# Streaming a two-layer transformer's weight matmuls backwards, with interleaved stationary columns

## What is computed

```
proj = rmsnorm(x) @ w_in                    # 2048 x 7184, then the two mixers
x = x + mixed @ w_out
x = x + cross_attention(rmsnorm(x), rmsnorm(mem), w_xq, w_xkv, w_xo)
x = x + conv_ffn(rmsnorm(x), w_up, w_down)  # 2048 x 11264, 5632 x 2048
p = rmsnorm(x) @ fox_w_in; x = x + (fox_attention(p) * silu(gate)) @ fox_w_out
p = rmsnorm(x) @ swa_w_in; x = x + (swa_attention(p) * silu(gate)) @ swa_w_out
```

## Time and profile before

| | |
|---|---|
| runs | 2170.38, 2169.81, 2169.99 us |
| median | 2169.99 us |
| profiled execution | span 2167.6 us from its first to its last instruction; what lies around the span is the 2.4 us to the median |
| TensorE busy | 2156.3 us, 99% |
| weight loads busy | 1865.8 us, 86% (beside the matmuls) |
| VectorE, ScalarE busy | 75%, 61% |
| DMA | 389 MB, mean 180 GB/s |

### The profile page before, as it was taken

How to read it: one execution, slowest core, us unless ns; L and a number is a source line. 1 busy time by engine, 2 the same in 40 slices (tenths; PEclk the granted TensorE clock), 3 DMA queues, 4 the chain that set the end, 5 groups by cost and what they waited for, 6 DMA issues and landing times.

```text
span 2167.6 us, 34503 instructions
## 1 busy us (share of the span) xinstructions
PE 2156.3 (99%) x13406; PEld 1865.8 (86%) x13406; DVE 1618.3 (75%) x2945; ACT 1327.2 (61%) x2601; POOL 9.7 (0%) x22
## 2 busy tenths in 40 slices
PE   9999999999999999999999999999999999999998
PEld 8888888888888888888888888888888888888887
DVE  7898666786688877655778867777676767688774
ACT  7866447775576666544666656555556655567764
POOL 0000000000000000000000000000000000000000
PEclk9999999999999999999999999999999999999999
DMA  7443434665455555555555555545554455544453
GB/s 279 169 146 137 147 115 141 218 217 186 156 190 189 188 191 186 193 185 192 187 191 189 185 194 185 193 171 197 181 177 174 167 192 186 189 161 155 146 200 140
DMA packets 107619, 389.31 MB, mean 180 GB/s; under 512 B 12304, under 2 KB 12560, under 8 KB 106688
## 3 DMA queue, kind: packets, MB, share of 16 engines
q1 hardware_dynamic: 105264, 377.31, 50.2%
q0 software_dynamic: 1904, 9.47, 1.2%
q10 hardware_dynamic: 288, 0.32, 0.0%
HBM read 384.34 MB, written 2.13 MB: 178 GB/s over the span
## 4 chain that ended last, share of the span: by engine, by line
PE 95%; DVE 3%; ACT 1%; issue 0%; DMA 0%; SPq 0%; DVEq 0%; ACTq 0%
PE main L510 88%; PE two L510 6%; PE two L513 1%; DVE WL L987 1%; DVE gt L987 0%; DMA RAW<-ws 0%; DVE GQ L993 0%; ACT L1654 0%; ACT WH L1655 0%; DVE GK L993 0%; PE main L556 0%; ACT PP L1655 0%; DVE PB L987 0%; ACT NT L1655 0%; DVE PP L993 0%
## 5 line engine op out<-in xcount | busy, mean ns | idle before, releaser
L1655 ACT ACTIVATE WH<-RAW 128x512 fp32r<-128x512 f32 x1416 | 882.1, 629 | 657.6 <-PE main L510 651.1
L987 DVE TENSOR_TENSOR WL<-RAW,WH 128x512 fp32r<-128x512 f32 x1416 | 961.2, 687 | 383.9 <-ACT WH L1655 374.4
L510 PE MATMUL main<-A,WH 128*128 128x512 f32 (+1 forms) x3680 | 1141.9, 393 | 1.0 <-DVE WL L987 1.0
L510 PEld LDWEIGHTS main<-A,WL 128*128 128x128 f32 x3584 | 673.9, 188 | 154.8
L510 PE MATMUL main<-A,WL 128*128 128x256 f32 x3584 | 713.7, 278 | 0.0
L510 PEld LDWEIGHTS main<-A,WH 128*128 128x128 f32 x3680 | 562.7, 189 | 13.8 <-issue 9.3
L510 PE MATMUL main<-H,WH 128*128 128x512 f32 x704 | 221.1, 395 | 0.0
L510 PE MATMUL main<-B,WH 128*128 128x512 f32 (+1 forms) x640 | 184.4, 373 | 0.0
L510 PEld LDWEIGHTS main<-H,WL 128*128 128x128 f32 x704 | 132.3, 188 | 31.3
L510 PE MATMUL main<-H,WL 128*128 128x256 f32 x704 | 138.4, 278 | 0.0
L510 PE MATMUL main<-WH,A 128*128 128x512 f32 (+1 forms) x448 | 137.6, 380 | 0.0
(11 more groups left out here) (322 smaller groups left out, 1722.5 us busy)
## 6 DMA issues: line engine op xcount, KB each, us to landing
RAW<-ws SPq DMA_DIRECT2D x707, 512.0 KB, 3.3
CB<-cscr POOLq DMA_DIRECT2D x4, 1024.0 KB, 4.7
XT<-xT POOLq DMA_DIRECT2D x4, 512.0 KB, 6.0
MS<-memT POOLq DMA_DIRECT2D x4, 512.0 KB, 8.7
xs<-xT SPq DMA_DIRECT2D x7, 256.0 KB, 7.6
out<-YT SPq DMA_DIRECT2D x7, 256.0 KB, 2.6
CST<-cst SPq DMA_DIRECT2D x1, 1248.0 KB, 7.9
G<-g POOLq DMA_DIRECT2D x1, 1024.0 KB, 5.9
```

Source lines behind the costliest of these rows:

```text
L510: return e.matmul(o, l, r, start=start, stop=True, skip_group_check=True)
L987: return e.tensor_tensor(o, a, b, op)
L1655: return e.activation(o, i, f, bias=bias, scale=scale, accum_out=accum)
```

## The change

`back` reverses the moving operand and the result of a matmul along their columns, and replaces `mm` in every matmul of `main(j)` except the transposes of `w2*`. Both are reversed, so each result column lands where it did. In the forms other than tokens, a stationary operand is now every second column of a block of 256 (`fblock`), and the host puts the columns of the weights in that order beforehand (`PLACE`), so the same 128 columns are loaded in the same order as before. Neither the stationary operand of tokens nor the order of instructions changes.

```
+def fblock(b):
+
+    return slice(256 * (b // 2) + b % 2, 256 * (b // 2) + 256, 2)
+
+
+PLACE = np.array([256 * (_f // 256) + 2 * (_f % 128) + _f // 128 % 2 for _f in range(512)])
...
+        for part in range(parts_of(key)):
+            if form_of(key, part) != "tokens":
+                n = k // 2 // parts_of(key)
+                halves = out[at + part * n:at + part * n + n].reshape(128 * n, 2, 512)
+                halves[:, :, PLACE] = halves.copy()
...
+            def back(o, l, r, start=True):
+                return mm(o[:, ::-1], l, r[:, ::-1], start)
...
-                        cols = [slice(256 * r + 128 * t, 256 * r + 128 * t + 128) for t in range(2)]
+                        cols = [fblock(2 * r + t) for t in range(2)]
                         for t in range(2):
-                            mm(P[:, t, :], h[:, cols[t]], both, start=first and r == 0)
+                            back(P[:, t, :], h[:, cols[t]], both, start=first and r == 0)
                         for t in range(2):
-                            ins = mm(P[:, t, 0:T], l[:, cols[t]], hi, start=False)
+                            ins = back(P[:, t, 0:T], l[:, cols[t]], hi, start=False)
...
                             hi, lo = (X[:, kt, a, 128 * t:128 * t + 128] for a in range(2))
-                            mm(P[:, t, 0:n], hi, h[:, cols], start=first and r == 0)
-                            mm(P[:, t, 0:n], hi, l[:, cols], start=False)
-                            ins = mm(P[:, t, 0:n], lo, h[:, cols], start=False)
+                            back(P[:, t, 0:n], hi, h[:, cols], start=first and r == 0)
+                            back(P[:, t, 0:n], hi, l[:, cols], start=False)
+                            ins = back(P[:, t, 0:n], lo, h[:, cols], start=False)
...
-                        cols = slice(128 * r, 128 * r + 128)
-                        mm(o, h[:, cols], X[:, kt, 0, :], start=first and (r == 0 if form == "small" else r % 2 == 0))
-                        mm(o, l[:, cols], X[:, kt, 0, :], start=False)
-                        ins = mm(o, h[:, cols], X[:, kt, 1, :], start=False)
+                        cols = fblock(r)
+                        back(o, h[:, cols], X[:, kt, 0, :], start=first and (r == 0 if form == "small" else r % 2 == 0))
+                        back(o, l[:, cols], X[:, kt, 0, :], start=False)
+                        ins = back(o, h[:, cols], X[:, kt, 1, :], start=False)
```

More of the change, by code:

```diff
@@ L576, in main @@
                             kh, kl = (W[:, (j - i + kt) % NW, :] for W in (WH, WL))
-                            mm(P[:, t, :], hi, kh, start=False)
-                            mm(P[:, t, :], hi, kl, start=False)
-                            ins = mm(P[:, t, :], lo, kh, start=False)
+                            back(P[:, t, :], hi, kh, start=False)
+                            back(P[:, t, :], hi, kl, start=False)
+                            ins = back(P[:, t, :], lo, kh, start=False)
                         if i == n - 1 and t == 0:
```

## The result

Slower, by little: median 2198.77 us (2198.57 to 2200.53, four runs) against 2170.03 us, ratio 1.0134 with an interval of 1.012 to 1.0149. That lies inside the stated range (2040 to 2215), but the forecast was 2091, a gain of 79 us, and the kernel lost 28.7 us.

What follows compares the result with a forecast made beforehand. TensorE, busy 99% of the span with back-to-back matmuls, was taken as the bound. 83 us saved in the wide form's 512-column slots, less 4 given back, made 79: 2170 - 79 = 2091 us, range 2040 to 2215.

Steps and rivals of the forecast that it cites:

- The bound and the excess: TensorE's back-to-back matmuls in `main`: spacing of starts sets the time, 14.2 ns too many per wide-form matmul.
- the 4 us given back to VectorE: Between 108 and 163 us VectorE is nearly always busy, so 4 us of the gain were taken off.
- (c): Wide form, reversal and step 2 together: load and moving streams at one pace should cross once, then keep apart.
- the first term of the sum: Wide form's 512-column slots lose their 19.5 ns excess except 2.1 ns: 4768 slots, 83 us saved.
- The bare handover of 2.1 ns: Excess left per 512-column wide slot, estimated from eight transposes at 108.8 ns each, if streaming at TensorE's lower level.
- Part (a): Moving operand and result last to first in all `main` matmuls: at best 158 us gained (2012), at worst columns take double.
- tokens at nothing with ends 0 and 16 us: Tokens form, whose stationary operands keep their step: no gain counted, possible gain between 0 and 16 us.
- rival 3: Columns backwards stream at half pace, in reading or writing, in `main`: 1813 us more, 3983 in all; chance 0.04.
- Part (b): Stationary operands at every second column in wide, plain, small: at best relieves the streams' meeting, at worst loads at half pace.
- rival 2: Step-2 weight load slows 256-column slots once it grows over 11 ns: 2275 at 20% more, 2716 at half pace; chance 0.20.
- Rival 1: All `main` matmuls: excess is a fixed handover, or direction and step are neutral or undone: 2170; chance 0.18.
- The 256-column slots: Short slots of the wide form, about as long as their load: expected unchanged, a pair staying at 0.23 us.

Runs made afterwards that it cites:

- e6: Kernel before the change, with every moving operand repeating its first column (products no longer the reference's): 2074.7 us.
- e5: Kernel before the change, with each weight load of the down projections reading its first column 128 times: 2170.8 us.
- e1: Changed kernel with stationary operands contiguous again, so only moving operand and result are reversed: 2196.53 us, ratio 1.0122.
- e3: Kernel before the change, with only the moving operand read backwards and results written forward (columns land mirrored): 2197.1 us.
- e4: Kernel before the change, with only the result written backwards and the moving operand read forward (columns land mirrored): 2169.93 us.
- e2: Changed kernel with directions turned forward again, so only stationary operands at every second column remain: 2184.55 us, ratio 1.0067.
- e14: Kernel before the change, with first and third matmul of a wide quad, plain and small backward, the rest forward: 2191.02 us, ratio 1.0096.
- e9: Kernel before the change, with each wide quad ordered long, short, long, short instead of long, long, short, short: 2186.64 us, ratio 1.0076.
- e8: Kernel before the change, with stationary operands at every fourth column (products are of other columns): 2796.24 us.

## Why the prediction was wrong

**The bound and the excess** held. The spacing of starts sets the time, and 14.2 ns for each matmul beyond its columns was there to be won or enlarged: with a read that stays, 95 us go (e6). Waits took no part in the loss, but for the start of the profiled execution; the 4 us given back to VectorE were not needed. Such a price exists, though: in e6, where TensorE does get faster, the chain between 18 and 30 us runs over ScalarE and VectorE.

**The step that failed is (c) and the first term of the sum**: "the 512-column slots of the wide form lose their excess", 83 us saved. They kept all of it: two of them take 0.47 us in the rows after, 469.2 ns in the mean where it was 465.9. The ground for it was the uneven split of the excess among slots of one size, from which I took a meeting of the load's stream with the read's at different paces. Holding the load still shows that the load's travel is worth 3.3 of 56.7 ns (e5), and giving both streams one pace saved nothing. The uneven split is real, but it comes with the moving operand's travel: with the read still it is gone, 5.0 ns in either size (e6). That one stream alone could make the excess, and cost more when it is turned round, stands nowhere in the prediction.

**The bare handover of 2.1 ns** in the same term is shown by no row. It supposes that the eight transposes stream at 1.2 GHz, while the granted clock of that window is 1.00. The nearest that the runs show is what is left with the read still, 5.0 ns a matmul in a quad and 3.0 in tokens. That these are of the same size as 2.1 is luck.

**Part (a), reading backwards**, was bounded at 2012 below and by half pace above, and taken as neutral in itself. It is worth +10.0 ns a quad and +6.2 ns a tokens slot, 26.7 us in the whole kernel (e1), all in reading (e3, e4). I had put tokens at nothing with ends 0 and 16 us on the side of a gain; it is some 6 us on the other side. That the time still fell inside the range is luck: its upper end was set by a slower load, which is not what cost here. The real price was a small cost that none of my rivals named: rival 3 has the direction but at half pace, +1813 us.

**Part (b), step 2**, was nearest to rival 2. Its mechanism is there in e2, where a load of WL lengthened from 188 to 194 ns and a short pair from 230.8 to 235.6 (+6.6 a quad, 14.7 us in all), and at step 4 it becomes what the rival's half pace described: 2796 us measured, 2716 worked out there for loads of twice the length that long slots still hold, which they did not. But the threshold was wrong. I let the load grow by 11 ns for free; it shows as 194 and 196 ns in e2 (WL and WH), 6 to 7 more than before, and already cost. And in the kernel as changed the term doesn't show, as the reversal hides it.

**Rival 1** (fixed handover) was wrong as the reason for the whole excess: two thirds of it vanish with the read's travel. For what is left then it may hold, since 660.1 - 640 = 20 ns a quad are 5 ns a matmul whatever its columns; but a tokens slot keeps only 3.0.

**The 256-column slots** I expected to stay. They took most of the loss: the short pair went from 230.8 to 237.5 ns, so the sign that I gave for rival 2 (a pair above 0.25 us) was set too wide to see it.

**Open**: why travelling costs 6 ns more per 512 columns backward; what the third of the excess is that stays with the read still; why a quad stands at 706.7 ns in the mean after four different edits (all backward, half backward, another order, backward with shifted weights), though single quads differ (706 or 707 ns in after, 702 to 711 in e14, 699 to 711 in e9); why a shift by 32 bytes costs tokens 4 ns a slot and a wide quad nothing in the mean.

## What to carry to other kernels

Where TensorE is bound by matmuls back to back, read the spacing of starts from an unbroken stretch of the chain and take the columns at the granted clock from it; what is left can be dissected by holding one operand still. Leave moving operands ascending, and keep weights in the order in which they are loaded: in this kernel fp32 weights at step 2 cost 0.7% (e2), at step 4 they cost 29% (e8). The direction of the result in PSUM was free (e4), so where an order has to be turned, turn it there.

## What the runs showed of the hardware that I had not expected

- In tokens form a moving operand that travels over SBUF costs 11 ns per 512 fp32 columns more than one within 16 bytes (227.2 against 216.3 ns a slot), whether it covers 2 KB or 1 KB twice.
- With a moving operand that stays on one column a matmul of a wide quad takes 5.0 ns more than its columns, with 512 of them as with 256.
- Backwards the travel costs 17 ns. In the plain form, with slots of 256 columns, backwards is the cheaper by 1.7 ns (118.3 against 120.0, e1).
- Prices of patterns don't add up: +10.0 (backward) and +6.6 (step 2) together make +10.0 ns a quad.
- Interchanging two matmuls of a quad, with the same operands and columns, costs 10.0 ns in the unbroken stretch (e9); whether for the order of lengths or for two results in a row in one bank is open. The whole grew by 16.6 us, less than the 23.8 that 2384 quads would make, so not every quad pays it.
